# A two-layer decoder trunk on one core: the last of a layer's eight plain up-projection tiles in two token halves

## The chip, the cores and the metric

One NeuronCore of a Trainium2 chip runs the whole program. The metric is the device time of one execution in microseconds (us). Five engines matter: TensorE (PE) does the matmuls and its weight loads (PEld in the rows), VectorE (DVE), ScalarE (ACT) and GpSimd (POOL) do the element-wise work, SyncE (SP) issues the DMAs. Engines wait for each other by semaphores, which the code counts up (`then_inc`) and waits for (`wait_ge`).

## The reference

Input x has 512 tokens of 1024 features, float32. Two layers follow each other, the first with an mLSTM mixer, the second with sliding-window attention. Each layer ends in a gated MLP, and that is where the change is:

```python
def conv_ffn(h, w_up, conv_w, conv_b, w_down):
    u = h @ w_up                                   # 1024 -> 2 * 2816
    gate, val = jnp.split(u, 2, axis=-1)
    gp = jnp.pad(gate, ((0, 0), (CONV_W - 1, 0), (0, 0)))
    gate_c = conv_b + sum(conv_w[j] * gp[:, j:j + S] for j in range(CONV_W))
    return (jax.nn.silu(gate_c) * val) @ w_down
```

Before and after every sub-layer stands an RMSNorm, and the sub-layer's result is added to the stream.

## The kernel before, in words

**Numbers as pairs.** Every projection splits both operands into a high part and the rest (`act_hi`, `act_lo`; `held_hi`, `held_lo`) and sums three products: high weights with high activations, high with low, low with high. ScalarE makes the high parts with a cast copy, VectorE the low parts with a subtraction.

**Units.** A unit of weights is 128 output features by 1024 input features. It is loaded by one DMA of 512 KB, split, and held in one of eight slots. `project(g, bank, lo, hi)` (L1860) computes unit g for the tokens lo to hi: for each of 8 blocks k of 128 inputs it issues three matmuls (L1865, L1866, L1867), each with its own weight load, into PSUM bank `bank`, columns lo to hi. That is 24 matmuls of hi - lo columns. The whole width S is 512, the half HT is 256.

**Where the operands lie.** A slot has 1024 columns of 4 bytes. `w_hi` and `w_lo` are the eight slots from the tensors' start. `on_hi` and `on_lo` (L144) are the same eight slots moved by STEP = 48 columns, 192 bytes. `held(g)` (L403) takes the moved ones if g is in the set STEPPED (L102), which holds all units of the first mixer and the first half of its output projection, units 6 and 7 of each layer's up-projection, and some others. Ahead of `act_hi` in memory lie `held_hi` (8448 columns) and `held_lo` (8240 columns), so `act_hi` begins 66752 bytes behind `held_hi`, and 66752 = 130 x 512 + 192. `act_lo` and the four sums of activations that the loop below uses lie at the same place modulo 512 bytes. Block k of a unit's weights begins k x 512 bytes into its slot, block k of the activations k x 2048 bytes in, and the second token half 1024 bytes further.

**The up-projection.** A layer has 22 tiles of 128 hidden features; each has a gate unit and a value unit. The first four tiles (PLAIN = 4, so 8 units, numbers 0 to 7 in slots 4, 5, 6, 7, 4, 5, 6, 7) are projected plainly. PE does in `ffn` (L2085): the first token halves of units 0 to 3, then the second halves of units 0 to 3, then units 4 to 7 at full width (L2098 to L2103), units 6 and 7 being gate and value of tile 3, in banks 2 and 3. At the end of each unit it counts `w_used` up once. All these units are of the project lines.

**The loop behind it.** The other 18 tiles are computed with seven block products instead of eight: sums of weights (GpSimd, L629 to L634) and sums of activations are multiplied. `product` (L2110) issues 12 matmuls of 256 columns (L2117, L2118, L2119); seven products make a tile, two tiles a pass of the loop, nine passes 1512 matmuls. Its weights lie in the slots without the shift. Between products, parts of PSUM are copied by ScalarE (`part`, L913, copy at L919) and added by VectorE; the fourth product of a tile waits for the second copy (`part_done`).

**Who waits for unit 7.** GpSimd's first sums for tile 5 write a slot that unit 7 used and wait for its count (L629); their last piece is split by VectorE at L1577, which the second product of tile 5 needs. VectorE's `gated_val` (L1511, operation at L1517) multiplies the value in bank 3 with the activated gate and waits for it too. The convolution of tile 3 (ScalarE L879, VectorE L1503 and L1507, ScalarE's SiLU L873) waits for unit 6 alone. The order of work in each engine's queue is written out by hand.

**After the loop** comes the down-projection (`down_part`, L2145), 512 columns per matmul.

Of the kernel before, what the change touches and what calls it, by code (L numbers as in the profile page):

```python
# [39 lines left out]
def trunk(nc, x, x_turned, columns, m_w_in, m_gate_bias, m_w_out, a_w_in, a_sinks, a_w_out,  # L40
          a_b_out, norm_mix_pre, norm_mix_post, norm_ffn_pre, norm_ffn_post, f_w_up, f_w_down, out):
    S, D = x.shape[1], x.shape[2]
# [32 lines left out]
    PLAIN = 4  # L75
# [3 lines left out]
    HT = S // 2  # L79
# [43 lines left out]
    def counted(g):  # L123
        return g + 1 + CREDIT

    with ExitStack() as ctx:
# [3 lines left out]
        def sem(name):  # L130
            return ctx.enter_context(nc.semaphore(name))
# [136 lines left out]
        w_hi_done, w_lo_done, w_used = sem("w_hi_done"), sem("w_lo_done"), sem("w_used")  # L268
# [138 lines left out]
        def by_tile(g):  # L407
            return [w.rearrange("p (k c) -> p k c", k=KT) for w in held(g)]
# [1450 lines left out]
        def _(pe):  # L1859
            def project(g, bank, lo=0, hi=S, ks=range(KT)):  # L1860

                uh, ul = by_tile(g)
                for k in ks:
                    dst, zh, zl = ps[:, bank, lo:hi], act_hi[:, k, lo:hi], act_lo[:, k, lo:hi]
                    nc.tensor.matmul(dst, uh[:, k], zh, start=(k == 0), stop=False)  # L1865
                    nc.tensor.matmul(dst, uh[:, k], zl, start=False, stop=False)  # L1866
                    ins = nc.tensor.matmul(dst, ul[:, k], zh, start=False, stop=(k == KT - 1))  # L1867
                return ins
# [216 lines left out]
            def ffn(l, blocks_done, turn_last):  # L2085


                up, down = G_UP[l], G_DOWN[l]
# [9 lines left out]
                for n in range(2, PLAIN):  # L2098
                    t = n % 2
                    pe.wait_ge(hid_done, l * FT + n + 1)  # L2100
                    for q in range(2):
                        pe.wait_ge(w_lo_done, counted(up + 2 * n + q))
                        project(up + 2 * n + q, 2 * t + q).then_inc(w_used, 1)  # L2103

                z1a, z2a, z2b = ([[a[:, k0 + k, b * HT:(b + 1) * HT] for a in (act_hi, act_lo)] for k in range(KT // 2)]
                                 for k0, b in ((0, 0), (KT // 2, 0), (KT // 2, 1)))
# [17 lines left out]
                with pe.Fori(PLAIN // 2, FT // 2) as m:  # L2124
                    for t in range(2):
                        n = l * SEVENS + t - PLAIN
# [46 lines left out]
                for b in range(NB - l):  # L2173
                    for s in range(TAIL):
                        if b == 0:
                            n = FT - TAIL + s
# [21 lines left out]
            def norm_blocks(n):  # L2198
                pe.wait_ge(moved_lo, min(n, FIRST_MOVED))
                if n == NB:  # L2200
                    pe.wait_ge(z_lo, NB - FIRST_MOVED)

            ffn(0, norm_blocks, lambda: turn_norm(2 * NB - 1, NB - 1, 6))


# [159 lines left out]
            def turned_blocks(n):  # L2365
                pe.wait_ge(moved_lo, len(MOVED))
                if len(TURNS) > 2 * (NB - n):
                    pe.wait_ge(t_lo, len(TURNS) - 2 * (NB - n))

            ffn(1, turned_blocks, lambda: [work(w) for w in LAST])  # L2370


# [38 lines left out]
```

## Time and profile before

| what | us |
|---|---|
| median of 3 runs | 1049.85 |
| lowest and highest run | 1043.26, 1057.09 |
| profiled execution, its own time | 1055.57 |
| its span, first to last instruction | 1053.8 |
| PE busy | 1043.9 |
| VectorE, ScalarE, GpSimd busy | 721.4, 543.9, 291.5 |

The profile is of one execution. The span is 1.8 us less than that execution's own time. PE's busy time is the time in which at least one matmul is under way; single matmuls overlap, since the next one starts before the one ahead has left the array. So their pace is read from the distance of their starts, not from their durations. In a timeline row the first number is the start in us from the span's start, the second the duration in us, then engine, line, operation, output and inputs, shape and count, and in brackets an idle time before it with what ended it.

### The profile page before, as it was taken

The numbers are of one execution on the slowest core, as the hardware profiler recorded it, in microseconds if no ns is written. First come the engines' busy times: TensorE is split into PE (matmuls) and PEld (weight loads), VectorE is DVE, ScalarE is ACT, GpSimd is POOL, SyncE is SP. The second block draws the span as 40 slices with busy tenths as digits, with TensorE's granted clock in tenths as the row PEclk, the third lists the DMA queues.
The fourth block names the chain that finished last, engine by engine and source line by source line (L and its number), as shares of the span: only waits on it lengthen the run. The fifth ranks groups of instructions, "written<-read, shape, count | busy, mean of one in ns | idle before, by whom it ended". The sixth has DMA issues, their size and how long they took to land.

```text
span 1053.8 us, 18751 instructions
## 1 busy us (share of the span) xinstructions
PE 1043.9 (99%) x6822; PEld 934.2 (89%) x6822; DVE 721.4 (68%) x1011; ACT 543.9 (52%) x974; POOL 291.5 (28%) x195
## 2 busy tenths in 40 slices
PE   9999999999999999999999999999999999999997
PEld 8888888898999999988889987779999999988886
DVE  7544578679888888633366587778988888843344
ACT  6511447355666666422345376754666666632242
POOL 1000211004676676100000023202467667500000
PEclk9999999999999999999999999999999999999999
DMA  9342328332344343122272552123234334223331
GB/s 280 105 133 80 100 81 251 49 99 83 100 119 113 86 119 119 60 86 94 100 200 61 143 117 81 21 60 100 58 103 119 102 97 119 80 80 100 100 140 80
DMA packets 154828, 111.18 MB, mean 106 GB/s; under 512 B 35536, under 2 KB 140144, under 8 KB 154784
## 3 DMA queue, kind: packets, MB, share of 16 engines
q1 hardware_dynamic: 153776, 107.41, 35.5%
q0 software_dynamic: 864, 2.92, 0.9%
q8 instruction: 28, 0.46, 0.2%
q10 hardware_dynamic: 144, 0.26, 0.1%
q14 instruction: 16, 0.13, 0.0%
HBM read 106.87 MB, written 2.13 MB: 103 GB/s over the span
## 4 chain that ended last, share of the span: by engine, by line
PE 94%; DVE 3%; ACT 1%; SPq 1%; issue 0%; DMA 0%; POOL 0%; DVEq 0%
PE ps L2118 11%; PE ps L2117 11%; PE ps L2119 11%; PE ps L2151 8%; PE ps L2150 8%; PE ps L2152 8%; PE ps L1865 6%; PE ps L1867 6%; PE ps L1866 6%; PE ps L2056 2%; PE ps L2058 2%; PE ps L2057 2%; PE ps L1945 1%; PE ps L1946 1%; PE ps L1947 1%; PE ps L2247 1%
## 5 line engine op out<-in xcount | busy, mean ns | idle before, releaser
L1865 PE MATMUL ps<-act_hi,held_hi 128*128 128x256 f32 (+1 forms) x440 | 143.4, 326 | 1.3 <-DVE act_lo L1195 1.2
L1867 PE MATMUL ps<-act_hi,held_lo 128*128 128x256 f32 (+1 forms) x440 | 141.0, 320 | 0.0
L1866 PE MATMUL ps<-act_lo,held_hi 128*128 128x256 f32 (+1 forms) x440 | 140.9, 320 | 0.0
L2117 PE MATMUL ps<-act_hi,held_hi 128*128 128x256 f32 x432 | 121.4, 281 | 0.0
L2119 PE MATMUL ps<-act_hi,held_lo 128*128 128x256 f32 x432 | 121.4, 281 | 0.0
L2118 PE MATMUL ps<-act_lo,held_hi 128*128 128x256 f32 x432 | 121.4, 281 | 0.0
L1656 DVE TENSOR_TENSOR held_lo<-raw,held_hi 128x1024 fp32r<-128x1024 f32 x32 | 39.2, 1225 | 117.9 <-ACT held_hi L982 117.9
L629 POOL TENSOR_TENSOR sums<-raw 128x512 f32<-128x512 f32 x36 | 50.1, 1390 | 238.8 <-DMA raw<-in_f_w_up 117.0
L2152 PE MATMUL ps<-held_hi,held_lo 128*128 128x512 f32 x288 | 112.1, 389 | 0.0
L2151 PE MATMUL ps<-held_lo,held_hi 128*128 128x512 f32 x288 | 112.1, 389 | 0.0
L2150 PE MATMUL ps<-held_hi 128*128 128x512 f32 x288 | 112.0, 389 | 0.0
L1577 DVE TENSOR_TENSOR held_lo<-sums,held_hi 128x1024 fp32r<-128x1024 f32 x72 | 88.0, 1225 | 26.0 <-POOL sums L634 18.8
L673 ACT CAST held_hi<-raw 128x1024 fp32r<-128x1024 f32 x66 | 68.1, 1044 | 64.4 <-PE ps L1947 24.7
L1140 DVE TENSOR_TENSOR held_lo<-raw,held_hi 128x1024 fp32r<-128x1024 f32 x73 | 88.0, 1220 | 19.3 <-ACT held_hi L673 18.2
L982 ACT CAST held_hi<-raw 128x1024 fp32r<-128x1024 f32 x32 | 33.8, 1055 | 122.3 <-PE ps L2152 122.3
L1865 PEld LDWEIGHTS ps<-act_hi,held_hi 128*128 128x128 f32 x440 | 82.6, 188 | 10.7 <-DVE act_lo L1195 1.7
L1866 PEld LDWEIGHTS ps<-act_lo,held_hi 128*128 128x128 f32 x440 | 82.7, 188 | 6.9 <-issue 0.2
L1867 PEld LDWEIGHTS ps<-act_hi,held_lo 128*128 128x128 f32 x440 | 82.6, 188 | 7.0
L907 ACT CAST held_hi<-sums 128x1024 fp32r<-128x1024 f32 x72 | 75.5, 1052 | 15.6 <-POOL sums L632 15.4
L2117 PEld LDWEIGHTS ps<-act_hi,held_hi 128*128 128x128 f32 x432 | 82.9, 192 | 0.1
L632 POOL TENSOR_TENSOR sums<-raw 128x512 f32<-128x512 f32 x36 | 82.1, 2280 | 0.0
L2118 PEld LDWEIGHTS ps<-act_lo,held_hi 128*128 128x128 f32 x432 | 81.1, 188 | 0.1
(266 smaller groups left out, 2833.1 us busy)
## 6 DMA issues: line engine op xcount, KB each, us to landing
raw<-in_f_w_up SPq DMA_DIRECT2D x88, 512.0 KB, 4.7
raw<-in_f_w_down SPq DMA_DIRECT2D x44, 512.0 KB, 3.3
raw<-in_m_w_in SPq DMA_DIRECT2D x23, 512.0 KB, 4.6
raw<-in_m_w_out SPq DMA_DIRECT2D x8, 512.0 KB, 3.3
raw<-in_a_w_in SPq DMA_DIRECT2D x16, 256.0 KB, 4.6
raw<-in_a_w_out SPq DMA_DIRECT2D x16, 256.0 KB, 4.7
h<-in_x SPq DMA_DIRECT2D x4, 512.0 KB, 7.5
h<-in_x_turned SPq DMA_DIRECT2D x3, 512.0 KB, 6.8
```

The source lines that it names most:

```text
L632: nc.gpsimd.tensor_tensor(lo[:, 3], val[:, first], gate[:, first], ALU.subtract).then_inc(s_sum, 1)
L1140: nc.vector.tensor_tensor(lo, raw[:, s % 4], hi.bitcast(F32), ALU.subtract).then_inc(w_lo_done, 1)
L1577: ins = nc.vector.tensor_tensor(lo, sums[:, t, fs], hi.bitcast(F32), ALU.subtract)
L1865: nc.tensor.matmul(dst, uh[:, k], zh, start=(k == 0), stop=False)
L1866: nc.tensor.matmul(dst, uh[:, k], zl, start=False, stop=False)
L1867: ins = nc.tensor.matmul(dst, ul[:, k], zh, start=False, stop=(k == KT - 1))
L2117: nc.tensor.matmul(dst, uh, zh, start=(start and k == 0), stop=False, skip_group_check=not start)
L2118: nc.tensor.matmul(dst, uh, zl, start=False, stop=False, skip_group_check=not start)
L2119: ins = nc.tensor.matmul(dst, ul, zh, start=False, stop=(k == KT // 2 - 1), skip_group_check=not start)
L2150: nc.tensor.matmul(dst, hi[:, bs], wh[:, hs], start=start, stop=False)
L2151: nc.tensor.matmul(dst, hi[:, bs], wl[:, hs], start=False, stop=False)
L2152: return nc.tensor.matmul(dst, lo[:, bs], wh[:, hs], start=False, stop=stop)
```

## The change

In both layers, unit 7 (the value unit of plain tile 3) is no longer projected with 24 matmuls of 512 columns but with 24 of columns 0 to 255 and then 24 of columns 256 to 511. The weights stay where they are, moved by STEP; the bank, the order of the three products and the one count of `w_used`, at the end of the second half, stay too. Nothing else is changed.

```diff
@@ -2100,7 +2100,11 @@
                     pe.wait_ge(hid_done, l * FT + n + 1)
                     for q in range(2):
                         pe.wait_ge(w_lo_done, counted(up + 2 * n + q))
-                        project(up + 2 * n + q, 2 * t + q).then_inc(w_used, 1)
+                        if 2 * n + q == 2 * PLAIN - 1:
+                            project(up + 2 * n + q, 2 * t + q, 0, HT)
+                            project(up + 2 * n + q, 2 * t + q, HT, S).then_inc(w_used, 1)
+                        else:
+                            project(up + 2 * n + q, 2 * t + q).then_inc(w_used, 1)
```

## Rows read from the trace of the kernel before

**Rows 1.** The page: span, busy time by engine, granted clock in 40 slices.

```profile
span 1053.8 us, 18751 instructions
...
PE 1043.9 (99%) x6822; PEld 934.2 (89%) x6822; DVE 721.4 (68%) x1011; ACT 543.9 (52%) x974; POOL 291.5 (28%) x195
...
PEclk9999999999999999999999999999999999999999
```

**Rows 2.** The page: the chain that ended last, by engine.

```profile
PE 94%; DVE 3%; ACT 1%; SPq 1%; issue 0%; DMA 0%; POOL 0%; DVEq 0%
```

**Rows 3.** Groups by line and shape: count, busy us, mean ns of one.

```profile
L2117 PE MATMUL ps<-act_hi,held_hi 128*128 128x256 f32 x432 | 121.4, 281 | 0.0
...
L1865 PE MATMUL ps<-act_hi,held_hi 128*128 128x512 f32 x168 | 66.6, 397 | 0.0
```

**Rows 4.** PE's timeline: first start of unit 7 and of the loop, both layers.

```profile
253.24 0.39 PE L1865 MATMUL ps<-act_hi,held_hi 128*128 128x512 f32 x1
...
258.68 0.28 PE L2117 MATMUL ps<-act_hi,held_hi 128*128 128x256 f32 x1
...
744.88 0.39 PE L1865 MATMUL ps<-act_hi,held_hi 128*128 128x512 f32 x1
...
750.32 0.28 PE L2117 MATMUL ps<-act_hi,held_hi 128*128 128x256 f32 x1
```

**Rows 5.** PE's timeline, layer 0: second halves of unit 0, then units 4 and 5.

```profile
225.71 0.28 PE L1865 MATMUL ps<-act_hi,held_hi 128*128 128x256 f32 x1
...
236.59 0.39 PE L1865 MATMUL ps<-act_hi,held_hi 128*128 128x512 f32 x1
...
242.19 0.39 PE L1865 MATMUL ps<-act_hi,held_hi 128*128 128x512 f32 x1
```

**Rows 6.** PE's timeline, first mixer: the last output-gate unit's two halves.

```profile
155.36 0.28 PE L1865 MATMUL ps<-act_hi,held_hi 128*128 128x256 f32 x1
...
157.04 0.28 PE L1867 MATMUL ps<-act_hi,held_lo 128*128 128x256 f32 x1
...
162.30 0.28 PE L1866 MATMUL ps<-act_lo,held_hi 128*128 128x256 f32 x1
...
163.86 0.29 PE L1867 MATMUL ps<-act_hi,held_lo 128*128 128x256 f32 x1
```

**Rows 7.** PE's timeline: around the fourth product, both layers, and the loop's last matmul.

```profile
262.80 0.28 PE L2119 MATMUL ps<-t_early,held_lo 128*128 128x256 f32 x1
263.06 0.39 PE L2117 MATMUL ps<-t_last,held_hi 128*128 128x256 f32 x1
263.29 0.29 PE L2118 MATMUL ps<-t_last,held_hi 128*128 128x256 f32 x1
...
436.90 0.28 PE L2119 MATMUL ps<-act_hi,held_lo 128*128 128x256 f32 x1
...
754.45 0.28 PE L2119 MATMUL ps<-t_early,held_lo 128*128 128x256 f32 x1
754.63 0.38 PE L2117 MATMUL ps<-t_last,held_hi 128*128 128x256 f32 x1
754.85 0.28 PE L2118 MATMUL ps<-t_last,held_hi 128*128 128x256 f32 x1
```

**Rows 8.** Timelines of GpSimd, ScalarE, VectorE and PE, 258 to 271 us.

```profile
258.92 2.36 POOL L629 TENSOR_TENSOR sums<-raw 128x512 f32<-128x512 f32 x1 [8.21 <-PE ps L1867]
...
261.60 0.63 ACT L873 ACTIVATE arena<-arena 128x512 f32<-128x512 f32 x1 [0.93 <-DVE arena L1507]
...
262.64 0.85 ACT L919 COPY parts<-ps 128x256 f32<-128x256 f32 x2
...
261.48 2.26 DVE L1564 TENSOR_TENSOR held_lo<-raw,held_hi 128x1024 fp32r<-128x1024 f32 x1
...
266.69 1.23 DVE L1577 TENSOR_TENSOR held_lo<-sums,held_hi 128x1024 fp32r<-128x1024 f32 x1 [0.91 <-POOL sums L634]
...
270.24 0.28 PE L2117 MATMUL ps<-t_third,held_hi 128*128 128x256 f32 x1
```

## The prediction

> **What bounds the kernel now.** I read the page's shares first: TensorE (PE) is busy for 1043.9 us of a span of 1053.8 us, at a granted clock in the top tenth in every slice [rows 1], that is the 2.4 GHz level throughout. The chain that ended last is PE work for 94% of the span [rows 2]. So a nanosecond more on PE is a nanosecond more at the end, unless PE would have waited there anyway.
>
> The durations can't be added up. A projection matmul of 512 columns lasts 397 ns by its mean, a product of the loop with 256 columns 281 [rows 3], but they overlap. What counts is the distance from one start to the next, which the timeline gives: a unit is 24 matmuls, so from its first start to the first start behind it there are 24 steps.
>
> The trace shows five such paces.
> - The unit that the change touches (512 columns, weights shifted by 48): 253.24 to 258.68 is 5.44 us in layer 0, 744.88 to 750.32 is 5.44 in layer 1, so 226.7 ns a matmul [rows 4].
> - The second halves of units 0 to 3 (256 columns, weights not shifted): 225.71 to 236.59 is 10.88 us for 96 matmuls, 113.3 ns each; then unit 4 (512 columns, not shifted): 236.59 to 242.19 is 5.60 us, 233.3 ns each [rows 5].
> - The last output-gate unit of the first mixer, the only unit in the trace that is both shifted and halved: 155.36 to 157.04 is 1.68 us for 14 steps and 162.30 to 163.86 is 1.56 us for 13 steps, 120 ns each in both halves [rows 6].
> - The loop of seven products behind the plain units (256 columns, not shifted): 18 tiles of 84 matmuls, from 258.68 [rows 4] to 436.90 [rows 7] 178.22 us for 1511 steps, less a stop of 0.25 (below), 117.8 ns each.
>
> So whether the shift helps depends on the width. By the tensor sizes in the code, an activation operand starts 192 bytes past the weights' place modulo 512 bytes; the shift of 48 columns is those 192 bytes and puts both in step. In step, 512 columns go at 226.7 instead of 233.3 ns, but 256 columns at 120 instead of 113.3.
>
> **The change, part by part.** Removed, in each of two layers: 24 matmuls of 512 columns with 24 weight loads, 5.44 us of PE time. Added: 48 matmuls of 256 columns with 48 weight loads. The shifted weights stay shifted, so the nearest row is the output-gate unit, which has the same helper, the same activation tensors and the same shift: 48 x 120 = 5.76 us. The lower end is the pace of the unshifted halves, 48 x 113.3 = 5.44 us, a difference of nothing. The upper end is a matmul whose weights weren't loaded ahead: the one at 263.06 holds its successor until 263.29, 0.23 us [rows 7], and 48 x 0.23 = 11.04 us, +5.60 us a layer. I take +0.32 us a layer, because both stretches of shifted halves stand at 120 once under way, and because no stretch of 256 columns [rows 5 to 7], stops aside, is slower than that. A gain below 5.44 has no row: no 256-column pace is under 113.3.
>
> The bank, the sums and the increment of w_used are as before, with the increment after the second half. There is no new wait, no DMA, nothing on other engines. What comes later by 0.32 us is what that increment releases: GpSimd's weight sums start at 258.92, released by this unit [rows 8], and would start at 259.24. Their last piece feeds the DVE split at 266.69, which waited for GpSimd [rows 8]; it would start near 267.0 and end near 268.2, and the product that needs it begins at 270.24 [rows 8]. That is 2.0 us of cover. VectorE's gating of the unit's tile also waits for the increment, but in the order of its queue it stands behind the weight split that begins at 261.48 and runs to 263.7 [rows 8].
>
> **What is late next.** Inside the first pass of the loop PE stops once. In layer 0 the fourth product should follow 262.80 by 0.12 and starts at 263.06; its second matmul comes 0.23 later instead of 0.12. That is 0.14 + 0.11 = 0.25 us lost. In layer 1 it is 754.45 to 754.63 and then to 754.85, 0.06 + 0.11 = 0.17 us [rows 7]. PE waits for ScalarE's copy of a part, the first of the two from 262.64, and ScalarE was late since it waited for VectorE's convolution tap before its 261.60 [rows 8]: a chain of ScalarE and VectorE work on gate tile 3, on unit 6 and not on unit 7. It stays where it is when PE comes 0.32 us later, so PE finds the part ready and both stops go. Net: layer 0 0.32 - 0.25 = +0.07, layer 1 0.32 - 0.17 = +0.15, together +0.22 us.
>
> The Trainium skill, "TensorE: Matmul & The Clock Gate", What happens when you issue a matmul, says that TensorE has two independent SBUF read ports and that loading the next weights takes nothing from the running matmul. By that the shift of 48 columns could not matter and only a small fixed cost per matmul would be left: its section Back-to-back issue gap gives N/2.4 + 2.5 ns, and 24 more matmuls would be +0.06 us a layer as an estimate from that page, which the stop in the loop would swallow. The trace disagrees on the first point: 233.3 against 226.7 ns with nothing but the shift between units 4 and 7.
>
> **Against the times.** The profiled execution took 1055.57 us with a span of 1053.8. With +0.22 it is 1055.8, a ratio of 1.0002. On the median of the runs, 1049.85 us, that is 1050.1 us. The profile lies 5.7 us above the median, and the runs spread from 1043.26 to 1057.09, which is 30 times the change and more. I note that the three runs lie 6.6 and 7.2 us apart, and that one layer's loop at 113.3 instead of 117.8 ns would be 1511 x 4.5 ns = 6.8 us. No row shows the loop at that pace, but a stretch with the same weights' places (slots 4 to 7) and activations did run at it [rows 5].
>
> **The rivals.**
> - *Slower: the loop changes its pace.* The loop behind the unit is 3022 steps, so what happens there outweighs the unit. If PE enters it from shifted halves and its loads and streams keep the slower order, at 120 instead of 117.8 ns, that is 3022 x 2.2 = 6.7 us, and the stops are worth no more than 0.42: 1049.85 + 6.9 = 1056.8 us. It decides as soon as the loop's pace moves by 0.1 ns (0.3 us). For it: the same operand places have two paces in this trace (113.3 in the halves, 117.8 in the loop). Against it: after each stop in the loop [rows 7] the old pace is back within some matmuls, in both layers.
> - *Faster: the same, the other way.* The loop takes on 113.3 ns: 3022 x 4.5 = 13.6 us less, with the +0.2 of the unit 1036.5 us. The same evidence.
> - *No difference.* The halves run at 113.3, the unit costs 5.44 as before and the stop stays: 1049.85 us. For it, the eight unshifted halves at that pace; against it, the output-gate unit.
> - *Placement doesn't matter and a step costs a little more:* below 0.1 us a layer, covered by the stop: 1049.85 us.
> - *Loads not hidden:* 2 x 5.60 less 0.42 = +10.8 us, 1060.7 us. Against it are some 3,000 steps of 256 columns with loads hidden.
>
> **How the numbers follow.** Forecast 0.62, no difference by pace 0.12, placement without effect 0.07, loop slower 0.08, loop faster 0.08, loads not hidden 0.03. The predicted time is the forecast's, 1050.1 us. Its own uncertainty from the paces is less than 0.7 us, but what is measured is a median of runs that spread over 14 us. So the range goes from 1042.5, under the lowest run, to 1058.0, which takes in the slower loop and the highest run; the faster loop at 1036.5 and the unhidden loads at 1060.7 stay out, 0.11, and scatter has the rest. About 2% is what a measurement of this kernel can tell from no change, 21 us. No case gets there: 0.02 for faster, 0.02 for slower for what I have not seen, 0.96 within.
>
> **What would show it right or wrong.** In the timeline of the changed kernel the touched unit should take 5.76 us (48 starts 0.12 apart) in both layers; 5.44 speaks for "no difference". The fourth product of the loop should start without a stop, 0.12 behind its forerunner, near 263.0 in layer 0; if the stop is still there, ScalarE's chain did depend on this unit. The loop should take 178.0 us per layer; 181 or 171 would be a changed pace and make the prediction wrong in its main point. The number of project matmuls of 256 columns should rise by 96 and of 512 columns fall by 48 over the three lines.

## The result, and the profile after

The changed kernel takes 1056.84 us (median of 22 runs, 1055.91 to 1058.54), the kernel before 1050.36 us in the same session (22 runs, 1043.15 to 1058.15). The ratio is 1.0047 with a 95% interval of 1.0027 to 1.0066: slower by about half a per cent. The whole interval lies above 1, and the change is within the 2% that I called no change. The forecast was 1050.1.

The medians hide the main thing. The 22 times of the kernel before stand at three levels: 2 under 1044, 12 from 1049 to 1051, 8 above 1055. All 22 of the changed kernel stand at the upper one. Over all sessions of this study the kernel before was timed 108 times beside other kernels: 31 at the lower level, 56 at the middle, 21 at the upper. The levels are 6 to 7 us apart. So the change didn't add 6 us to anything; it took away the two quicker outcomes.

The profiled executions are both from the upper level (1055.57 and 1056.57 us), and there the change looks as harmless as forecast. From the page and the groups by shape of the changed kernel (count, busy us, mean ns of one, idle before):

```profile
span 1054.8 us, 18847 instructions
PE 1045.1 (99%) x6870; PEld 937.5 (89%) x6870; DVE 721.0 (68%) x1011; ACT 543.8 (52%) x974; POOL 290.1 (28%) x195
...
L1865 PE MATMUL ps<-act_hi,held_hi 128*128 128x256 f32 x304 | 85.8, 282 | 1.1 <-DVE act_lo L1195 1.1
```

PE has 48 more matmuls than in [rows 1] and is 1.2 us longer busy; the other engines have the same instructions and are busy as long to within 1.4 us. PE's timeline of the changed kernel, which answers to [rows 4] and [rows 7]:

```profile
254.09 0.28 PE L1865 MATMUL ps<-act_hi,held_hi 128*128 128x256 f32 x1
...
259.84 0.28 PE L2121 MATMUL ps<-act_hi,held_hi 128*128 128x256 f32 x1
...
263.97 0.28 PE L2123 MATMUL ps<-t_early,held_lo 128*128 128x256 f32 x1
264.08 0.28 PE L2121 MATMUL ps<-t_last,held_hi 128*128 128x256 f32 x1
...
437.81 0.28 PE L2123 MATMUL ps<-act_hi,held_lo 128*128 128x256 f32 x1
...
745.75 0.28 PE L1865 MATMUL ps<-act_hi,held_hi 128*128 128x256 f32 x1
...
751.50 0.28 PE L2121 MATMUL ps<-act_hi,held_hi 128*128 128x256 f32 x1
...
929.47 0.28 PE L2123 MATMUL ps<-act_hi,held_lo 128*128 128x256 f32 x1
```

Unit 7 takes 5.75 us in both layers (254.09 to 259.84, 745.75 to 751.50), 119.8 ns a matmul. The fourth product follows its forerunner by 0.11 us: the stop is gone. The loop's last start in layer 1 of the kernel before was this:

```profile
928.46 0.28 PE L2119 MATMUL ps<-act_hi,held_lo 128*128 128x256 f32 x1
```

From unit 7's start to the loop's end it is 183.72 us in both layers, where before it was 183.66 (253.24 to 436.90) and 183.58 (744.88 to 928.46): +0.06 and +0.14, forecast +0.07 and +0.15. Nearly all the rest of the 1.0 us between the two spans lies ahead of unit 7 of layer 0 (0.85 us), where nothing was changed.

So the same profile comparison that confirms the sum can't show where the half per cent comes from. That needs executions from the other levels.

### The profile page after: what moved, and what is told of

The parts are those of the page before. It is cut to its first block, busy times and chain, and to the rows that moved or that the text cites. A ratio compares the mean times of both kernels' runs of the same rounds, so it can differ in the third digit from the quotient of the medians.

```text
span 1054.8 us, 18847 instructions
## 1 busy us (share of the span) xinstructions
PE 1045.1 (99%) x6870; PEld 937.5 (89%) x6870; DVE 721.0 (68%) x1011; ACT 543.8 (52%) x974; POOL 290.1 (28%) x195
## 4 chain that ended last, share of the span: by engine, by line
PE 94%; DVE 3%; ACT 1%; SPq 1%; issue 0%; DMA 0%; POOL 0%; DVEq 0%
PE ps L2122 11%; PE ps L2121 11%; PE ps L2123 11%; PE ps L2154 8%; PE ps L2156 8%; PE ps L2155 8%; PE ps L1865 6%; PE ps L1867 6%; PE ps L1866 6%; PE ps L2056 2%; PE ps L2058 2%; PE ps L2057 2%; PE ps L1945 1%; PE ps L1947 1%; PE ps L1946 1%; PE ps L2251 1%
## 5 line engine op out<-in xcount | busy, mean ns | idle before, releaser
L1865 PE MATMUL ps<-act_hi,held_hi 128*128 128x256 f32 (+1 forms) x456 | 146.2, 321 | 1.2 <-DVE act_lo L1195 1.1
L1867 PE MATMUL ps<-act_hi,held_lo 128*128 128x256 f32 (+1 forms) x456 | 143.8, 315 | 0.0
L1866 PE MATMUL ps<-act_lo,held_hi 128*128 128x256 f32 (+1 forms) x456 | 143.8, 315 | 0.0
L1656 DVE TENSOR_TENSOR held_lo<-raw,held_hi 128x1024 fp32r<-128x1024 f32 x32 | 39.2, 1225 | 117.9 <-ACT held_hi L982 117.9
L673 ACT CAST held_hi<-raw 128x1024 fp32r<-128x1024 f32 x66 | 68.1, 1044 | 64.8 <-PE ps L1947 24.7
L1865 PEld LDWEIGHTS ps<-act_hi,held_hi 128*128 128x128 f32 x456 | 85.8, 188 | 10.0 <-DVE act_lo L1195 1.5
L1866 PEld LDWEIGHTS ps<-act_lo,held_hi 128*128 128x128 f32 x456 | 85.9, 188 | 6.4 <-issue 0.2
L1867 PEld LDWEIGHTS ps<-act_hi,held_lo 128*128 128x128 f32 x456 | 85.8, 188 | 6.3
L2121 PEld LDWEIGHTS ps<-act_hi,held_hi 128*128 128x128 f32 x432 | 82.9, 192 | 0.0
L907 ACT CAST held_hi<-sums 128x1024 fp32r<-128x1024 f32 x72 | 75.5, 1051 | 14.3 <-POOL sums L632 14.3
L2123 PEld LDWEIGHTS ps<-act_hi,held_lo 128*128 128x128 f32 x432 | 81.1, 188 | 0.0
```

The lines of the kernel that those rows point to most:

```text
L2121: nc.tensor.matmul(dst, uh, zh, start=(start and k == 0), stop=False, skip_group_check=not start)
L2123: ins = nc.tensor.matmul(dst, ul, zh, start=False, stop=(k == KT // 2 - 1), skip_group_check=not start)
```

## The experiments

A ratio is a run's time to that of the kernel before, timed beside it in the same session, with a 95% interval in brackets. The kernel before mixes three levels, and their shares differ between sessions (8 of 22 at the upper level in the first, none of 13 in the last), so a ratio near one says little. Which levels a kernel's runs stand at says more.

**Again: what are the levels?** The kernel before, unchanged, twice.

> The kernel before, unchanged, for its spread of times and for a second profile. Its runs so far stand at three levels, near 1043, 1050 and 1057 us, the profiled one at the upper with both layers' loops at 117.8 ns a step. Theory A (the product loop has two paces, 113.3 and 117.8 ns, and each layer's loop takes one of them by execution): the levels show again, and a profiled execution near 1050 shows exactly one layer's loop near 113.3 ns (1511 steps x 4.5 ns = 6.8 us), one near 1043 both. Rival B (the levels come from elsewhere, from the start of the program or its first loads): a profile near 1050 or 1043 shows both loops at 117.8 ns and another stretch shorter by 6.8 us.

Ten runs: one at 1043.3, seven from 1048.78 to 1049.93, two at 1055.69 and 1056.13; median 1049.24, ratio to the kernel before 0.9995 [0.9957, 1.0033]. The profiled one was again from the upper level (1055.69), with both loops at 117.8. In its layer 0 there was no stop at all: the plain second halves ahead had come at 117.8 ns too (225.67 to 236.97, 96 matmuls in 11.30 us against 10.88 in [rows 5]), so PE was 0.42 us later from that stretch alone, and the fourth product followed by 0.12 us:

```profile
263.19 0.28 PE L2119 MATMUL ps<-t_early,held_lo 128*128 128x256 f32 x1
263.31 0.28 PE L2117 MATMUL ps<-t_last,held_hi 128*128 128x256 f32 x1
```

The kernel before can lose its stop by itself, then. A further execution was profiled later.

> The kernel before, one look, to catch an execution at the middle or lower level in a profile. If its time is near 1050: exactly one layer's loop near 113.3 ns, with the pace at 117.8 up to a stop and 113.3 behind it. If near 1043 both. If near 1056 neither.

It took 1042.75 us. Its PE timeline at the loop's first start, around the fourth product, and at the loop's last start, both layers:

```profile
258.96 0.28 PE L2117 MATMUL ps<-act_hi,held_hi 128*128 128x256 f32 x1
...
263.08 0.28 PE L2119 MATMUL ps<-t_early,held_lo 128*128 128x256 f32 x1
263.34 0.38 PE L2117 MATMUL ps<-t_last,held_hi 128*128 128x256 f32 x1
...
430.63 0.28 PE L2119 MATMUL ps<-act_hi,held_lo 128*128 128x256 f32 x1
...
744.07 0.28 PE L2117 MATMUL ps<-act_hi,held_hi 128*128 128x256 f32 x1
...
748.20 0.28 PE L2119 MATMUL ps<-t_early,held_lo 128*128 128x256 f32 x1
748.38 0.39 PE L2117 MATMUL ps<-t_last,held_hi 128*128 128x256 f32 x1
...
915.67 0.28 PE L2119 MATMUL ps<-act_hi,held_lo 128*128 128x256 f32 x1
```

Ahead of the stop the pace is the old one: 35 steps in 4.12 us, 117.7 ns. Behind it 1475 steps take 167.29 us in both layers, 113.4 ns. In the first profile the same stretch, 263.06 to 436.90 [rows 7], took 173.84. That is 6.55 us a layer and 13.1 for both; the times differ by 12.8 (1055.57 to 1042.75). That fits theory A: each layer's loop runs at one of two paces, and the levels are none, one or both loops at the quick one. No profile of the kernel before fell on the middle level; layer0_only below has one at 1049.7 us, with one quick loop. And the profile names the place: the pace changes at the stop.

**No stop, with the unit at full width.**

```diff
+                        if 2 * n + q == 2 * PLAIN - 1:
+                            uh = by_tile(up + 2 * n + q)[0]
+                            for k in range(2):
+                                nc.tensor.matmul(ps[:, 2 * t + q, 0:S], uh[:, k], act_hi[:, k, 0:S], start=True, stop=True)
                         project(up + 2 * n + q, 2 * t + q).then_inc(w_used, 1)
```

> Unit 7 at full width as in the kernel before, with two further matmuls of 512 columns ahead of it (products of two blocks, overwritten by the unit): 2 x 226.7 ns = +0.45 us of PE work a layer, which is more than the stop ahead of the fourth product needs to vanish. Net +0.90 - 0.42 = +0.5 us. Theory A1 (the loop gets the chance of the quick pace from the stop in its first pass; without a stop it keeps 117.8): all runs in the upper level, 1057 to 1058 us, none near 1050 or 1043. Theory A2 (it is the pace of the unit ahead that decides; 512 columns in step leave the chance, halves in step at 120 ns take it away): three levels as before, at 1044, 1051 and 1058, median about 1051.

1056.89 us, ten runs from 1056.06 to 1058.06, ratio 1.008 [1.0047, 1.0113]. Not one quick run, without any halving: 0.45 us of delay a layer does what the change did. Its timeline in layer 0, from the loop's first start to its last:

```profile
259.82 0.28 PE L2121 MATMUL ps<-act_hi,held_hi 128*128 128x256 f32 x1
...
263.94 0.28 PE L2123 MATMUL ps<-t_early,held_lo 128*128 128x256 f32 x1
264.06 0.28 PE L2121 MATMUL ps<-t_last,held_hi 128*128 128x256 f32 x1
...
437.78 0.28 PE L2123 MATMUL ps<-act_hi,held_lo 128*128 128x256 f32 x1
```

The fourth product follows by 0.12 us, and 1511 steps take 177.96 us, 117.8 ns.

**The stop back, with the unit in halves.** In the changed kernel PE waits one copy longer ahead of the fourth product, in a layer's first pass only.

```diff
                         pe.wait_ge(part_done, m * 8 + 4 * n + 2)
+                        if t == 0:
+                            pe.wait_ge(part_done, 4 * l * SEVENS + 3)
                         product(t, 2, t4, gate, first, False).then_inc(product_mm, 1)
```

> The changed kernel, with PE waiting for the third copied part already before the fourth product, in the first pass of each layer alone (the wait is on a constant, later passes find it met): a stop of 0.3 to 0.5 us comes back where the change had removed it. The entry is still from halves in step at 120 ns. A1 (the stop gives the chance): levels near 1043.5, 1050.5 and 1057.5 appear again, median below 1055. A2 (the unit ahead decides): all runs at 1057 to 1058 us, the changed kernel's 1056.8 plus 0.6 to 1.0.

1044.8 us, nine of ten runs from 1043.89 to 1045.77 and one at 1051.35; ratio 0.996 [0.9919, 1.0001], though the halves are still there. The levels didn't just come back; the lower one became the rule. In layer 0's timeline the stop stands between these two starts, and the profile names the copy:

```profile
263.70 0.28 PE L2123 MATMUL ps<-t_early,held_lo 128*128 128x256 f32 x1
264.54 0.36 PE L2121 MATMUL ps<-t_last,held_hi 128*128 128x256 f32 x1 [0.55 <-ACT parts L919]
```

0.84 us from start to start instead of 0.12. My guess of 0.3 to 0.5 us for its length was low. With no_stop this separates the two things that the change does: halves with a stop are quick, full width without one is slow. But this stop is longer than the one that the change removed (0.26 and 0.18 us from start to start).

**The same stop alone**, in the kernel before.

> The kernel before (unit 7 at full width) with the longer stop alone: ahead of the fourth product of the first pass PE also waits for the third copied part. A1 (a stop of some 0.7 us makes the loop take 113.3 ns whatever stood ahead): nearly all runs at the lower level, the former 1044.8 with the halves less 2 x 0.32 = 1044.2 us, both loops at 113.3 ns in the profile. If the halves at 120 ns are part of the cure: three levels as in the kernel before, median near 1050.

1045.09 us, all ten runs from 1043.5 to 1046.9, ratio 0.9949 [0.992, 0.9977]. A second series:

> full_stop again, with more rounds, since its place above both kernels rests on 10 runs: a median of 1045 us, nearly all runs between 1043 and 1047, ratio to the kernel before near 0.995. If its quick loops were luck: some runs at 1050 or 1057.

1044.59 us, six runs from 1043.77 to 1045.16, ratio 0.9953 [0.9909, 0.9997]. Sixteen of sixteen runs at the lower level; the profiles of both series show both loops at 113.3 ns behind the stop. The timeline of the first series' profile:

```profile
264.05 0.28 PE L2119 MATMUL ps<-t_early,held_lo 128*128 128x256 f32 x1
264.88 0.36 PE L2117 MATMUL ps<-t_last,held_hi 128*128 128x256 f32 x1 [0.55 <-ACT parts L919]
265.08 0.28 PE L2118 MATMUL ps<-t_last,held_hi 128*128 128x256 f32 x1
...
432.13 0.28 PE L2119 MATMUL ps<-act_hi,held_lo 128*128 128x256 f32 x1
```

264.88 to 432.13 is 167.25 us, the quick pace. The stop costs 0.8 us a layer (0.83 and then 0.20 from start to start, 0.12 each without it) and saves 6.6. So this version lies below the median of the kernel before by half a per cent, and below every run of the changed kernel, by one wait and no work. It is no quicker than the kernel before at its own lower level (1042.2 to 1044.1 us).

**The change in layer 0 alone.**

```diff
-                        if 2 * n + q == 2 * PLAIN - 1:
+                        if l == 0 and 2 * n + q == 2 * PLAIN - 1:
```

> The change in layer 0 alone, layer 1 as in the kernel before. A (each layer's loop takes its pace by itself): layer 0's loop always at 117.8 ns, layer 1's as often quick as before, so two levels, near 1050 and 1057, and none at 1043. If the change acted on the program as a whole: all runs at 1057. The profile shows layer 0's loop without a stop and at 117.8.

1050.74 us; six of ten runs from 1049.48 to 1050.77, four from 1057.18 to 1059.18, none at the lower level; ratio 1.0036 [0.9996, 1.0076]. The profile (1049.7 us) has no stop and 117.8 ns in layer 0; in layer 1:

```profile
755.15 0.28 PE L2123 MATMUL ps<-t_early,held_lo 128*128 128x256 f32 x1
755.33 0.38 PE L2121 MATMUL ps<-t_last,held_hi 128*128 128x256 f32 x1
...
922.62 0.28 PE L2123 MATMUL ps<-act_hi,held_lo 128*128 128x256 f32 x1
```

167.29 us behind the stop. The two starts are 0.18 us apart, and in [rows 7] the same two of layer 1 are 0.18 apart too (754.45, 754.63), but there the loop kept 117.8. So a stop of this kind is a new draw and not a cure, and to 0.01 us its length doesn't tell the outcome. The trace holds the starts to the nanosecond. By it the two starts of layer 1 are 185 ns apart where the loop stayed slow (the kernel before, and again), 180 and 179 where it became quick (again_look, layer0_only); in layer 0 they are 262 ns apart in the slow case and 253 in the quick one. Six stops are too few to make a rule of it.

**A stop at the loop's entry.**

```diff
                 pe.wait_ge(t_form_lo, 4 * (l + 1))
+                pe.wait_ge(w_used, counted(up + 7))
```

> The kernel before with one more wait: PE waits for its own unit 7 to be finished (its count of w_used) ahead of the loop, so it stops there, once a layer, for the drain of the last matmul and the first exposed weight load, 0.2 to 0.4 us. What the copies wait for then comes later, and the stop at the fourth product goes. If any stop of this length starts a new pace (A1 in its plain form): both loops at 113.3 ns in most runs, 1043 to 1045 us. If the length or the place of the stop matters (the unshifted stream only locks anew when it is stopped itself): three levels, or all at 1057.

1050.44 us: four of ten runs from 1044.24 to 1046.62, six from 1050.4 to 1052.9; ratio 0.9986 [0.9959, 1.0014]. By the levels, 14 of 20 loops were quick. In the profile (1044.24 us) both were, from their start on and with no second stop. Last matmul of unit 7 and first of the loop, layer 0 and layer 1:

```profile
259.49 0.39 PE L1867 MATMUL ps<-act_hi,held_lo 128*128 128x512 f32 x1
260.33 0.38 PE L2117 MATMUL ps<-act_hi,held_hi 128*128 128x256 f32 x1 [0.45 <-DVE held_lo L1577]
...
744.86 0.39 PE L1867 MATMUL ps<-act_hi,held_lo 128*128 128x512 f32 x1
745.69 0.38 PE L2117 MATMUL ps<-act_hi,held_hi 128*128 128x256 f32 x1 [0.44 <-DVE held_lo L1577]
```

From start to start it is 0.84 and 0.83 us where 0.23 is the pace, more than my 0.2 to 0.4. By the trace PE's own count was met at 259.93 in layer 0; then the loop's set-up on PE's sequencer followed in steps of 0.1 us up to the weight load at 260.33, which no matmul hid here. VectorE's split, which the brackets name, had ended 0.30 and 0.38 us before the restart. A stop elsewhere can change the pace too, then, but the outcome stays a draw, though this stop is as long as full_stop's. That rules out that any stop of 0.83 us is as good as full_stop's.

**A shorter stop, timed by PE itself.**

```diff
                         pe.wait_ge(part_done, m * 8 + 4 * n + 2)
+                        if t == 0:
+                            pe.wait_ge(product_mm, 6 * l * SEVENS + 3)
```

> The kernel before with a shorter stop in the first pass: ahead of the fourth product PE waits until its own third product is finished. That is the drain of a matmul and an exposed weight load, about 0.3 us a layer in place of the 0.8 of full_stop, and like there it is released by PE's own chain, so at a fixed distance from its last matmul. If any stop that PE itself times leads to 113.3 ns: all runs near 1044, 0.9 us below full_stop. If a stop is a new draw and its length or phase decides the outcome: a mix of levels 6.7 us apart, as with entry_wait (4 of 10 runs at the lower level, 6 at the middle one).

Neither a saving nor a mix: 1056.67 us, five of six runs from 1056.6 to 1057.22 and one at 1044.55; ratio 1.005 [0.9996, 1.0103]. Its profile, layer 0:

```profile
263.52 0.28 PE L2119 MATMUL ps<-t_early,held_lo 128*128 128x256 f32 x1
263.95 0.36 PE L2117 MATMUL ps<-t_last,held_hi 128*128 128x256 f32 x1
...
437.74 0.28 PE L2119 MATMUL ps<-act_hi,held_lo 128*128 128x256 f32 x1
```

173.79 us behind the stop. At this place, ahead of the fourth product, a stop timed by PE's own third product has nearly one outcome: 0.83 to 0.84 us from start to start leads to the quick pace in 25 of 26 runs (full_stop and stop_back), 0.43 to the slow one in 5 of 6. By the trace these stops repeat to a nanosecond between the layers of a profile (833 and 833, 832 and 832, 429 and 429). The stops that hang on VectorE's chain, whose distance from PE's matmuls differs between executions, lead to either. So does entry_wait's, which PE times too but which isn't the same in the two layers (840 and 831). So neither the length to 0.01 us nor who times the stop tells the outcome. It may be a finer timing of the restart, but no run here varied that by itself.

**Out of step ahead of the loop.** Units 6 and 7 leave the shifted set; unit 7 stays in halves.

```diff
-        STEPPED |= set(range(G_UP[l] + 6, G_UP[l] + 2 * PLAIN)) | set(range(G_DOWN[l] + FT - TAIL, G_DOWN[l] + FT))
+        STEPPED |= set(range(G_DOWN[l] + FT - TAIL, G_DOWN[l] + FT))
```

> The changed kernel with units 6 and 7 taken out of the shifted set: unit 6 at 512 columns out of step (233.3 ns, 5.60 us, +0.16 a layer), unit 7 in halves out of step at 113.3 ns (5.44 us, -0.32 a layer against the changed kernel). The loop is then entered from 113.3 ns. The units alone give 1056.8 - 0.3 = 1056.5 us, the stop again partly there. A2 (the pace of the unit ahead carries over): both loops at 113.3 ns, every run near 1043 us. A1 (the stop gives the chance): the three levels, as a stop of some 0.1 to 0.2 us is back. If the loop keeps 117.8 whatever stands ahead: all near 1056.5.

1050.18 us, three of ten runs from 1042.55 to 1043.26, seven from 1049.48 to 1052.31; ratio 1.0011 [0.9971, 1.0051]. The profile (1042.55 us) has both loops at 113.3 ns ahead of and behind stops of 0.24 and 0.19 us. Neither theory had it whole: with a stop in the loop, two levels. Whether the slow loops lost the pace at the stop or came in slow isn't shown, since no slow execution was profiled. The last run took the stop away from this kernel, by four spare matmuls ahead of unit 7.

```diff
+                            uh = by_tile(up + 2 * n + q)[0]
+                            for k in range(4):
+                                nc.tensor.matmul(ps[:, 2 * t + q, 0:HT], uh[:, k], act_hi[:, k, 0:HT], start=True, stop=True)
                             project(up + 2 * n + q, 2 * t + q, 0, HT)
```

> unshifted_halves with four further matmuls of 256 columns ahead of unit 7 (products of four blocks, overwritten by the unit), 4 x 113.3 ns = +0.45 us a layer, so that no stop is left in the loop's first pass. If a stream that isn't stopped keeps the pace with which it comes (halves out of step at 113.3, then the loop at 113.3), and only a stop can change it: the loop is at 113.3 wherever unit 7 is, so most or all runs at the lower level, 1042.7 + 0.9 - 0.4 = 1043.2 us. If the loop without a stop always falls to 117.8, whatever stands ahead: all runs near 1056.5. The slow loops of unshifted_halves (7 of 10 runs had one) would come from its stops in the first case.

1043.44 us: eight of ten runs from 1043.07 to 1044.99, two at 1051.62 and 1053.02; ratio 0.9971 [0.9941, 1.0002]. The profile fell on 1051.62, which is lucky, since it shows both cases. Second half of unit 7, first and last start of the loop, layer 0 and layer 1:

```profile
258.14 0.28 PE L1865 MATMUL ps<-act_hi,held_hi 128*128 128x256 f32 x1
...
260.97 0.28 PE L2124 MATMUL ps<-act_hi,held_hi 128*128 128x256 f32 x1
...
438.93 0.28 PE L2126 MATMUL ps<-act_hi,held_lo 128*128 128x256 f32 x1
...
750.57 0.28 PE L1865 MATMUL ps<-act_hi,held_hi 128*128 128x256 f32 x1
...
753.29 0.28 PE L2124 MATMUL ps<-act_hi,held_hi 128*128 128x256 f32 x1
...
924.53 0.28 PE L2126 MATMUL ps<-act_hi,held_lo 128*128 128x256 f32 x1
```

In layer 0 the half takes 2.83 us, 117.9 ns a matmul, and the loop 177.96, 117.8. In layer 1 it is 2.72, 113.3, and the loop 171.24, 113.3. Neither has a stop. So the loop is not slow by itself: out of step, a stream that isn't stopped keeps the pace it came with, and the plain halves have the same two paces. In layer 0 the pace is older than unit 7: the second halves of units 0 to 3 already took 117.8 ns (226.74 to 238.05, 96 matmuls in 11.31 us), and three full-width units out of step lie between.

**All four units out of step in halves, with the longer stop.** `if True:` in place of the condition on unit 7, the set as above, and the wait of stop_back.

> A candidate for a kernel that beats both: units 4 to 7 out of the shifted set and all in two halves (113.3 ns a step, 5.44 us each instead of 5.60, 5.60, 5.44 and 5.44, so -0.32 us a layer), with the longer stop of stop_back. Stop as there, 0.7 to 0.8 us a layer. If the stop settles both loops at 113.3 ns: 1044.2 - 0.6 = 1043.6 us in nearly all runs. If the unshifted halves themselves run at 117.8 in some executions, up to 0.4 us a layer more.

A miss: 1052.63 us, 1047.86 to 1063.32, ratio 1.0048 [1.0001, 1.0095]. Layer 0:

```profile
259.19 0.28 PE L2121 MATMUL ps<-act_hi,held_hi 128*128 128x256 f32 x1
...
263.16 0.28 PE L2123 MATMUL ps<-t_early,held_lo 128*128 128x256 f32 x1
265.35 0.36 PE L2121 MATMUL ps<-t_last,held_hi 128*128 128x256 f32 x1 [1.92 <-ACT parts L919]
...
439.15 0.28 PE L2123 MATMUL ps<-act_hi,held_lo 128*128 128x256 f32 x1
```

PE came earlier by two times 0.16 us and waited for 2.19 us, as the chain of ScalarE and VectorE got later. The 35 steps ahead of the stop take 3.97 us, 113.4 ns; the 1475 behind it 173.80, 117.8. Here the stop lost the quick pace. In layer 1 of the same profile a stop of 2.12 us left the loop at 113.3. So a stop can change the pace in both directions. Several of the times (1055.99, 1058.38, 1063.32) fit no level, and no profile shows why.

## Why the prediction was right and wrong

- **The unit, +0.32 us a layer: right.** 5.75 against 5.76 us forecast, from the one unit that was both shifted and halved [rows 6].
- **What the count releases: right.** Nothing downstream came late; the product behind the GpSimd sums didn't wait.
- **"So PE finds the part ready and both stops go": right in itself, and the step that failed in its price.** I gave the going of the stops a worth of 0.25 + 0.17 us. Their going is what cost the time. The stop is where a loop that entered at 117.8 ns can change to 113.3, which is worth 6.55 us. Without it all 32 runs of the changed kernel and of no_stop stayed at the upper level.
- **The sum of 0.22 us: right for executions at the upper level, wrong for the median**, which moved by 6.5 us, since the median of the kernel before lies at the level of one quick loop. The loop's length was met as well: 177.96 us in the changed kernel, 178.0 forecast.
- **"The same operand places have two paces" and the distances of 6.6 and 7.2 us between the runs: right, and not followed up.** I took the loop's pace for a rival with 0.16 in all, on the ground that after each stop "the old pace is back". That rested on one execution, and on the level where it is true. The spread of the three runs, in steps of one loop, was the better evidence, and it should have carried the forecast: if the level is drawn somewhere, a change that touches the place of the draw can take it away.
- **The slower rival** named the size (1056.8 us, measured 1056.84) but by the wrong way: the loop never ran at 120 ns. It ran at the 117.8 of the profile, always instead of sometimes. The agreement of the number is an accident of which levels the median and the profile came from.
- **The range** held because it was set by the spread of the runs and not by the sum. That the median fell inside it is no evidence for the mechanism.

What stays open: why an unstopped stream out of step holds one of two paces, what in a restart picks it, and why layer 0's plain halves come at 117.8 ns in some executions (in 5 of the 14 profiles, layer 1's in none). It is shown that the loop's pace changes at a stop and nowhere else in these profiles; that fine timing picks the outcome is argued only.

## What to carry to other kernels

When the runs of one kernel stand at levels, find out what a level is before pricing a change: profile executions from two levels and compare start-to-start distances in the longest uniform stretch. A change of 0.3 us a layer moved the median by 6.5 us here, and between the outer levels it is 13, by removing a stop of PE at a certain place; the sum of instruction costs didn't show it. Here the best version is not the one with the least waiting: with one stop of 0.8 us a layer at the fourth product all 16 runs stood at the lower level. A different stop of the same length gave no such result, so such a stop has to be tried and not reckoned.

## What the runs showed of the hardware that I had not expected

- The same matmuls with the same operand places have two sustained paces, 113.3 and 117.8 ns for 256 columns, at a granted clock of 1.00 in both, each held over 1475 and more steps. The Trainium skill, "TensorE: Matmul & The Clock Gate", What happens when you issue a matmul, gives TensorE two independent read ports of SBUF, with nothing taken from the running matmul by the next weight load; this case's traces show a dependence on placement (226.7 or 233.3 ns for 512 columns, 120 or 113.3 for 256) and on history that this doesn't contain.
- Loops entered without a stop from operands in step, at 226.7 or at 120 ns, began at 117.8 in every profile (20 loops) and stayed there until a stop; six of them had none (both layers of the changed kernel and of no_stop, layer 0 of again and of layer0_only).
- In all_halves_stop the second of VectorE's two weight splits ahead of the stop took longer than before. VectorE's and GpSimd's timelines of that kernel:

```profile
258.58 3.46 DVE L1577 TENSOR_TENSOR held_lo<-sums,held_hi 128x1024 fp32r<-128x1024 f32 x2 [0.25 <-ACT held_hi L907]
```

```profile
259.44 1.53 POOL L629 TENSOR_TENSOR sums<-raw 128x512 f32<-128x512 f32 x1 [9.02 <-PE ps L1867]
```

The pair of splits took 3.46 us with a GpSimd sum started between them. In the kernel before the same pair took 2.36 (from 257.76), and there it was GpSimd's sum that took long, 2.36 us [rows 8] against 1.53 here. The Trainium skill, "SBUF — State Buffer", Who interferes with whom, says that a VectorE instruction with two SBUF inputs and a GpSimd instruction that reads SBUF exclude each other, the later one waiting. The trace agrees: 1.10 us longer on the one side, 0.83 shorter on the other. The order turned as well: GpSimd's sum, which waits for PE's unit 7, began 0.02 us behind the second split in the kernel before (258.90) and 0.29 us ahead of it here (259.73). So 0.32 us of shift between PE and the others lengthened PE's stop from 0.84 to 2.19 us; 0.84 + 0.32 + 1.10 is 2.26.
